# Differential attention with its scores as two 64-row tiles, query blocks that run on over the heads, a gathered rope, and the output gated from PSUM

## The reference, cut to what matters

```
aq, ak = rope_partial(a_q), rope_partial(a_k)      # 8 heads x 2 components x 64 dims, rope on the first 16 dims
s = einsum('bhcqd,bhckd->bhcqk', q, k) * 64 ** -0.5 # per head: two 1024 x 1024 score maps, contraction 64
p = softmax(s);  a = p[:, :, 0] - lam * p[:, :, 1]
o = a @ v                                           # v: 128 wide per head
o = rmsnorm(o, a_norm_g) * (1 - lam_init);  h_b = o * silu(a_z)
```

## Time and profile before

| | us |
|---|---|
| median of 3 runs | 1660.07 |
| the profiled execution, its own time | 1660.44 |
| its span on the core | 1658.4 |
| PE busy | 1600.7 (97%) |
| DVE, ACT, POOL busy | 985.6, 831.5, 542.7 |

### The profile page before, as it was taken

The page is one execution under the profiler, slowest core; times in us unless marked ns, Lnnn a source line. Parts: engine busy times, 40 slices in busy tenths (PEclk is TensorE's granted clock), DMA queues, the critical chain, the costliest instruction groups (busy, mean ns, idle before and its releaser), DMA issues.

```text
span 1658.4 us, 23808 instructions
## 1 busy us (share of the span) xinstructions
PE 1600.7 (97%) x8311; PEld 1338.9 (81%) x8311; DVE 985.6 (59%) x1607; ACT 831.5 (50%) x1474; POOL 542.7 (33%) x589
## 2 busy tenths in 40 slices
PE   6999999999999999999999999999999998999998
PEld 5788888888888878787777778787878887888898
DVE  6803774765665667777777777777776112334313
ACT  5314654654655654646464646555555234555312
POOL 4242152252161255151414233333310333333560
PEclk8999999999999999999999999999999999999999
DMA  5131021121121231212121212111211535432432
GB/s 164 34 121 39 26 88 39 55 72 38 51 74 29 66 87 29 58 32 58 32 57 32 57 32 57 32 44 32 53 60 32 181 114 165 152 92 86 127 102 102
DMA packets 130138, 116.08 MB, mean 70 GB/s; under 512 B 5210, under 2 KB 116379, under 8 KB 129060
## 3 DMA queue, kind: packets, MB, share of 16 engines
q1 hardware_dynamic: 125476, 102.78, 21.8%
q10 hardware_dynamic: 4608, 12.58, 2.0%
HBM read 85.96 MB, written 21.00 MB: 64 GB/s over the span
## 4 chain that ended last, share of the span: by engine, by line
PE 70%; DVE 10%; ACT 9%; issue 8%; DMA 2%; DVEq 0%; ACTq 0%; SPq 0%
PE ps L696 50%; PE ps L704 6%; PE ps L1002 6%; PE ps L908 2%; PE ps L900 2%; ACT aT_split L1903 2%; DVE aT_split L1437 2%; DMA k_stack<-k_stack 2%; DVE negmax L1432 2%; ACT probs L1898 1%; PE ps L785 1%; DVE state_f L1293 1%; ACT num L1801 1%; ACT w_split L1599 1%; PE ps L723 1%
## 5 line engine op out<-in xcount | busy, mean ns | idle before, releaser
L696 PE MATMUL ps<-xn_split,w_split 128*128 128x512 f32 x4224 | 1012.0, 396 | 0.4 <-DVE gate_cols L1198 0.4
L696 PEld LDWEIGHTS ps<-xn_split,w_split 128*128 128x128 f32 x4224 | 788.3, 189 | 166.6 <-DVE gate_cols L1198 0.6
L590 POOL TENSOR_TENSOR w_split<-w_raw,w_split 128x256 fp32r<-128x256 f32 x384 | 327.7, 884 | 956.9 <-ACT w_split L1599 956.3
L1898 ACT ACTIVATE probs<-ps,negmax 128x1024 f32<-128x1024 f32 x128 | 143.0, 1117 | 129.6 <-DVE negmax L1432 129.6
L1432 DVE TENSOR_REDUCE negmax<-ps 128x1 f32<-128x1024 f32 x128 | 150.0, 1212 | 2.4 <-PE ps L900 2.4
L1437 DVE TENSOR_TENSOR aT_split<-ps,aT_split 128x512 fp32r<-128x512 f32 x128 | 88.4, 691 | 100.8 <-ACT aT_split L1903 99.9
L900 PE MATMUL ps<-k_stack,q_stack 128*128 128x512 f32 x512 | 133.7, 403 | 2.8 <-DMA k_stack<-k_stack 2.7
L900 PEld LDWEIGHTS ps<-k_stack,q_stack 128*128 128x128 f32 x512 | 91.4, 188 | 20.9 <-issue 3.3
L704 PEld LDWEIGHTS ps<-aT_split,va_split 128*128 128x128 f32 x768 | 95.1, 190 | 10.6 <-issue 7.1
L704 PE MATMUL ps<-aT_split,va_split 128*128 128x256 f32 x768 | 98.8, 285 | 2.5 <-DVE aT_split L1437 1.9
L1599 ACT ACTIVATE w_split<-w_raw 128x1024 fp32r<-128x1024 f32 x94 | 98.9, 1052 | 0.2
(11 more groups left out here) (247 smaller groups left out, 1773.8 us busy)
## 6 DMA issues: line engine op xcount, KB each, us to landing
w_raw<-in_w_in SPq DMA_DIRECT2D x80, 512.0 KB, 3.9
k_stack<-k_stack SPq DMA_DIRECT2D x16, 512.0 KB, 4.2
qk_f<-spill_g SPq DMA_DIRECT2D x16, 512.0 KB, 3.6
spill_g<-qk_f ACTq DMA_DIRECT2D x12, 512.0 KB, 2.6
w_argument<-m_rows SPq DMA_DIRECT2D x8, 512.0 KB, 5.3
spill_m<-hT_f ACTq DMA_DIRECT2D x16, 256.0 KB, 2.2
spill_a<-o_out SPq DMA_DIRECT2D x32, 128.0 KB, 1.8
h_split<-spill_m SPq DMA_DIRECT2D x8, 512.0 KB, 5.0
```

What stands on the lines that cost most here:

```text
L590: lo = pool.tensor_tensor(wsp[b][:, 1, ks_], raw[b][:, ks_], wsp[b][:, 0, ks_].bitcast(F32), ALU.subtract)
L696: mm = pe.matmul(ps[:, half, :], wsp[b][:, wl, k, :], moving[:, xl, k, cols], start=(k == 0 and n == 0), stop=(k == KT - 1 and n == 2))
L1898: act.activation(pr[:, c], ps[:, 2 + 2 * c:4 + 2 * c, :].rearrange("p b k -> p (b k)"), ACT.Exp, bias=nmax[:, b, c:c + 1], accum_out=den[: ...
```

## The change

- Scores: `a_scores` (now also given which buffer) makes, per bank of 512 keys, three passes of high/low parts for each component, as matmuls over 64 rows: component 0 on partitions 0 to 63, component 1 on 64 to 127, one after the other into different banks. 12 matmuls per block, which wait for both exponentials of the block before.
- q and k are split whole (128 partitions at once) into two buffers each, one per parity of the head; the doubled copies and their DMA are gone. The loops over heads take two heads a turn.
- Order: the scores of the next head's block 0 stand in block 7 of this head. `fills` says how many steps of projection each block gets (10 and 6 in turn in a head that isn't the first), of which the first 3 stand between scores and the second round of transposes. Maxima and mixing of a head's block 0 go with its predecessor's block 7 on DVE and ACT.
- v's transposes go through banks 1 and 0 of the projections.
- Rope: four DMAs gather the 32 rows that turn from q (and from k) into a tile of 128 partitions x 2 x 128, POOL makes the rope on that, four DMAs give the rows back. cos and sin are loaded in that layout.
- Output: ACT squares it straight from PSUM, 1/rms is made in PSUM in place, DVE multiplies 1/rms, gain and gate, then the output from PSUM. The copy to `o_f32` is gone.
- Gate: its product is made by POOL in four pieces, the argument is clamped by DVE after block 0's work, and ACT's three steps stand at block 1. The mix's first half runs after the first exponential, its second half after the second.

```diff
+def fills(first):
+    return (0, 8) + tuple(8 + 14 * (q // 2) + 8 + 6 * (q % 2) for q in range(ST)) if first else \
+        (0, 0) + tuple(16 * (q // 2) + 10 + 6 * (q % 2) for q in range(ST))
+def halves(first, q):
+    at = fills(first)
+    return [n for n in range(8) if at[q + 1] < 8 * (n + 1) <= at[q + 2]]
...
-        qs = sb("q_stack", [P, 2, S], F32R, at=a_scope)
-        ks = sb("k_stack", [P, 2, 2, S], F32R, at=a_scope)
+        qs = [sb(f"aq_split{i}", [P, 2, S], F32R, at=a_scope) for i in range(2)]
+        ks = [sb(f"ak_split{i}", [P, 2, S], F32R, at=a_scope) for i in range(2)]
...
+            def turning(n, c, x):
+                rows = slice(c * AD + x * TURN, c * AD + (x + 1) * TURN)
+                return (qkf[rows, n].rearrange("i (b f) -> i b f", b=ST), turn_in[n][c * AD:(c + 1) * AD, x])
+            def gather(hh, n):
+                g, _ = tile_no(G_M, 8, MH - 1, 4 + n) if is_zero(hh) else tile_no(G_A, 4, hh - 1, n)
+                sp.wait_ge(proj_read, 2 * g + 2)
+                for c in range(2):
+                    for x in range(2):
+                        row, turn = turning(n, c, x)
+                        sp.dma_start(turn, row).then_inc(turn_gathered, 16)
+            def give_back(hh, n):
+                sp.wait_ge(turn_done, 4 * (2 * hh + n) + 4)
+                for c in range(2):
+                    for x in range(2):
+                        row, turn = turning(n, c, x)
+                        sp.dma_start(row, turn).then_inc(turn_returned[n], 16)
...
                 for j, c in enumerate((C_AQ, C_AK, C_AV, C_AZ)):
                     load_weights(G_A, 4, h, j, w_in_v, c + P + h * P)
-                    if j == (1 if first else 2):
-                        double_keys(h)
+                    if j < 2:
+                        gather(h, j)
+                        give_back(h, j)
                     if not first:
                         store_a(h - 1, j)
...
+                turn, own = 2 * hh + n, turn_in[n]
+                pool.wait_ge(turn_gathered, 64 * turn + 64)
+                pool.tensor_tensor(turn_cos, own, cos.unsqueeze(1).to_broadcast([P, 2, R_COLS]),
+                                   ALU.mult).then_inc(turn_done, 1)
+                for x in range(2):
+                    pool.tensor_tensor(turn_sin[:, x], own[:, 1 - x], sin[:, x], ALU.mult).then_inc(turn_done, 1)
+                pool.wait_ge(turn_done, 4 * turn + 3)
+                pool.tensor_tensor(own, turn_cos, turn_sin, ALU.add).then_inc(turn_done, 1)
+            def gate_product(h, first):
+                pool.wait_ge(a_gate_act.sem, a_gate_act.after(h, 2))
+                if not first:
+                    pool.wait_ge(a_ost.sem, a_ost.after(h, -1))
+                for n in range(QUARTERS):
+                    cols = slice(n * QUARTER, (n + 1) * QUARTER)
+                    g = pool.tensor_tensor(ga[:, cols], vz[:, 1, cols], aw[:, cols], ALU.mult)
+                g.then_inc(a_gate.sem, 1)
+            def a_tiles(h, first):
+                for j in range(3):
+                    split_weights(G_A, 4, h, j)
+                gate_product(h, first)
+                rope(h + 1, 0)
+                split_weights(G_A, 4, h, 3)
+                rope(h + 1, 1)
...
-            def a_scores(h, q):
+            def a_scores(h, par, q):
                 if q == 0:
-                    pe.wait_ge(k_doubled, 32 * h + 32)
-                    pe.wait_ge(a_qk_lo.sem, a_qk_lo.after(h, 3))
-                for c in range(2):
-                    if q > 0:
-                        pe.wait_ge(a_exp.sem, a_exp.after(h, 2 * (q - 1) + c))
-                    elif not is_zero(h):
-                        pe.wait_ge(a_exp.sem, a_exp.after(h, c) - 2)
-                    for i in range(2):
-                        for b in range(2):
-                            mm = pe.matmul(ps[:, 2 + 2 * c + i, :], qs[:, c, q * P:(q + 1) * P],
-                                           ks[:, c, b, i * HALF:(i + 1) * HALF], start=(b == 0), stop=(b == 1))
-                    mm.then_inc(a_score.sem, 1)
+                    pe.wait_ge(a_qk_lo.sem, a_qk_lo.after(h, 1))
+                if not (is_zero(h) and q == 0):
+                    pe.wait_ge(a_exp.sem, a_exp.after(h, 2 * q - 1))
+                for i in range(2):
+                    for n, (a, b) in enumerate(PASSES):
+                        for c in range(2):
+                            rows = slice(c * AD, (c + 1) * AD)
+                            mm = pe.matmul(ps[:, 2 + 2 * c + i, :], qs[par][rows, a, q * P:(q + 1) * P],
+                                           ks[par][rows, b, i * HALF:(i + 1) * HALF], start=(n == 0), stop=(n == 2))
+                            if i == 1 and n == 2:
+                                mm.then_inc(a_score.sem, 1)
...
+            def v_round(h, i, tile_half):
+                pe.wait_ge(proj_read, tile_half)
+                for n in range(4):
+                    c = 4 * i + n
+                    mm = pe.transpose(ps[:, 1 - i, n * P:(n + 1) * P], vz[:, 0, c * P:(c + 1) * P], ident[:])
+                mm.then_inc(a_vtr.sem, 1)
...
+            def a_head(h, par, first, last):
+                at = fills(first)
+                base, per_head, hh = (G_GL, 0, 0) if last else (G_A, 4, h)
+                def filler(begin, end):
+                    for n in range(8):
+                        lo, hi = max(begin, 8 * n), min(end, 8 * n + 8)
+                        if lo < hi:
+                            if lo == 8 * n and n in (1, 2):
+                                pe.wait_ge(a_vlo.sem, a_vlo.after(h, n - 1))
+                            proj_half(base, per_head, hh, n // 2, n % 2, begin=lo - 8 * n, end=hi - 8 * n)
+                read_by = 2 * (G_A + 4 * h)
                 if first:
+                    a_scores(h, par, 0)
+                    v_round(h, 0, read_by)
+                    filler(0, at[1])
                 for q in range(ST):
                     mix_round(h, q, 0)
                     if q + 1 < ST:
+                        a_scores(h, par, q + 1)
+                    elif not last:
+                        a_scores(h + 1, 1 - par, 0)
+                    if q == 0 and not first:
+                        v_round(h, 0, read_by)
+                    if q == (0 if first else 1):
+                        v_round(h, 1, read_by + 1)
+                    filler(at[q + 1], at[q + 1] + FIRST_PART)
                     mix_round(h, q, 1)
+                    if q == 0 and not first:
+                        squares(h - 1, 3)
                     if q % 2 == 0 and q > 0:
                         squares(h, q // 2 - 1)
+                    filler(at[q + 1] + FIRST_PART, at[q + 2])
                     if q % 2 == 1:
                         pv(h, q // 2)
+            a_head(0, 0, True, False)
+            with pe.Fori(0, AH // 2 - 1) as i:
+                a_head(2 * i + 1, 1, False, False)
+                a_head(2 * i + 2, 0, False, False)
+            a_head(AH - 1, 1, False, True)
...
+            def qk_low_a(hh, par, n):
+                dve.wait_ge(a_qk_hi.sem, a_qk_hi.after(hh, n))
+                dst = (qs, ks)[n][par]
+                dve.tensor_tensor(dst[:, 1], qkf[:, n], dst[:, 0].bitcast(F32), ALU.subtract).then_inc(a_qk_lo.sem, 1)
...
                 for q in range(ST):
+                    a_low_round(h, q, 0)
+                    nxt = (h, q + 1) if q + 1 < ST else None if last else (h + 1, 0)
+                    if nxt is not None:
+                        maxima(*nxt)
+                        mix_first(*nxt)
+                    a_low_round(h, q, 1)
+                    if q == 0 and not first:
+                        v_low_round(h, 0)
+                    if q == (0 if first else 1):
+                        v_low_round(h, 1)
+                    if nxt is not None:
+                        mix_second(*nxt)
                     if q == 0:
+                        dve.wait_ge(proj_read, 2 * (4 * h + G_A))
+                        if not first:
+                            dve.wait_ge(a_gate.sem, a_gate.after(h, -1))
+                        dve.tensor_scalar(aw, vz[:, 1], -1.0, LARGEST, ALU.mult, ALU.min).then_inc(a_clamped.sem, 1)
+                    if q == 1 and not first:
                         o_out_gate(h - 1, 3)
+                    if q in (3, 5, 7):
                         o_out_gate(h, q // 2 - 1)
+                    if q in (4, 6) and not last:
+                        qk_low_a(h + 1, 1 - par, q // 2 - 2)
...
                 for q in range(ST):
+                    nxt = (h, q + 1) if q + 1 < ST else None if last else (h + 1, 0)
+                    done = (h, q // 2 - 1) if q in (2, 4, 6) else (h - 1, 3) if q == 0 and not first else None
+                    high_round(h, q, 0)
+                    if done is not None:
+                        o_square(*done)
+                    if q == 0 and not first:
+                        v_high_round(h, 0)
```

(86 more changed lines are left out.)

364 lines of the change are left out of this document (119 added, 245 removed).

## The result

The changed kernel is slower: 1731.96 us, median of 4 runs (1729.56 to 1734.12), against 1658.62 us for the kernel before beside it; ratio 1.0443, 95% interval 1.0425 to 1.0461. Forecast were 1611 us and a range of 1589 to 1652.

What follows compares the result with a forecast made beforehand. TensorE's queue, busy 97% of the span, was taken to bound the kernel: 1660.4 - 29.6 (scores) - 35 (stops) + 17 (switches) - 1 (heads joined) = 1611.8, forecast 1611 us, range 1589 to 1652.

Steps and rivals of the forecast that it cites:

- (b): Stops within a head: filler between scores and second round of transposes leaves 1.0 of 5.4 us a head, -35 us.
- (e): Changed work of DVE, ACT, POOL and small DMAs, costed at nothing as lying beside TensorE's 78 us.
- (a): Scores: 512 matmuls of 128 rows become 384 pairs of 64 rows at 0.231 us a pair, -29.6 us.
- rival of serial pairs: Scores: the two 64-row matmuls run one after the other, 88.7 us over the forecast, 1700 us; chance 0.14.
- the one of loads that hold up the pairs: Scores: second tile's load not done beside the first's stream, +43 us, 1655 us; chance 0.06.
- (c): 128 switches between 128-row and 64-row work at 0.13 us each, +17 us.
- (d): Heads joined: next head's scores no longer wait at its start; 0.5 us ahead of head 0; -1 us.

Runs made afterwards that it cites:

- The three re-orderings: Kernel with gating moved early, with filler between the rounds, mix in halves and fillers of 10 and 6 all undone: 1641.32 us, ratio 0.9886.

## Why the prediction was wrong, point by point

- *The failed step is in (b), at the products with v.* I counted `pv`'s 2.89 us as cover for the mix, and never asked what `pv` itself waits for. The change swaps its wait from ACT's read (`a_rs`) to DVE's gating (`a_ost`), and the gating stands at the end of the odd block, behind the mix. That is readable in the code: `pv` of block 2n+1 wants what DVE does at the end of block 2n+1, ahead of which stand maxima and mix of block 2n+2. By the terms of (b) the price was there too: the mix ends 6.4 us after the scores, gating 0.9 later, 7.3, and `pv` was due 2.07 + 0.44 + 2.07 = 4.6 after them: 2.7 us, measured 2.3. The edit that its own title names, "gated from PSUM", I had put under (e), at nothing. Nor did I price that the change also puts the gating a block later. Moving the gating alone turned 1732 into 1620 us.
- *The clock wasn't in the sum.* No row of before had a stop of over 1 us within a head. But the trace of before shows elsewhere what a long one can do: in the tail TensorE stops for 4.6 us, and the granted clock of the next 4.6 us is 0.54. Here the clock took about a third of the loss.

```profile
1380.90 11.37 PE L696 MATMUL ps<-h_split,w_split 128*128 128x512 f32 x40 [4.64 <-DVE h_split L1507]
```

```profile
1380.90:1385.50 4.60, 4.60 (x12) 3.65 (x13) 0.00 (x0) 0.85 (x1) 0.93 (x2) 0.54 0.96 353
```

- *(a) was right as a mechanism*: pairs at one stream each, 12 matmuls in 1.58 us and not 2.8. The rival of serial pairs, which alone stood for "slower", is refuted, and so is the one of loads that hold up the pairs; the kernel was slower by a mechanism that no rival named.
- *(c) was too small*: 0.20 us a switch and not 0.13, 26 us and not 17. It lies within the bounds of 0 and 0.27 and nearer to the upper one, and eats nearly all of (a)'s 29.6 us. The Trainium skill's "Changing tiling mode (not just tile) drains the TensorE" ("TensorEngine Tiling (Array Packing)", Key Properties) gives no figure; that each switch costs 0.20 us here agrees with it.
- *The stops of (b), once gating is early*: work by the rows of before is 80.1 - 3.7 = 76.4 us a head, with switches 79.6; heads take 79.9. So 0.3 us of stops are left, not 1.0. The size was nearly right, the cause wrong: I gave it to the filler between the rounds, which alone is worth 5 us and in the kernel before less than nothing. The three re-orderings together carry 21 us, the rest of the change 18.
- *(d)*: the stops at the joined heads went, but TensorE's loop over a body of two heads costs 1.8 us at each of 2 turns, which I hadn't priced. The half us ahead of head 0 was not won: the first scores start at 603.2 as before, since TensorE, there 1.2 us earlier, waits 1.75 us for k's low part (DVE L1394), which (d) had hidden under the projections.
- With early gating the span is 1618.8, where (a) to (e) give 1609.8: + 9 for switches, + 3.6 for turns, + 1 for (d), - 5.6 for stops make 8 of the 9.

## What to carry to other kernels

When an edit drops a copy out of PSUM, the bank's release moves to the next reader: write down who releases each bank, and what stands ahead of that instruction in its engine's queue. Price every wait of the bounding engine anew, above all ahead of the work that the sum uses as cover. An engine that gets lighter (DVE, 65.7 to 57.7 us a head) can still become what everyone waits for, by order alone.

## What the runs showed of the hardware that I had not expected

- After 25 of 30 stops of 2.3 to 2.5 us TensorE ran for a while at the lower clock (in the one shown, granted 0.63 over the next 4.6 us), and 24 matmuls of 256 columns took 4.63 us instead of 3.04 to 3.13; after five it didn't, and the two stops of 1.6 and 1.8 us at the turns of the loop have no fall either. Useless matmuls in the stops made the kernel 35 us faster.
- Two 64-row matmuls on different rows run as one: in the changed kernel the two of a pair start 3 ns apart in the median and 20 at most, and 12 matmuls last 1.58 us, six streams and a switch. That holds (10 ns, 30 at most, and 1.59 us) also where the code lists three on one half of the rows and then three on the other. Going from 128-row to 64-row work or back costs 0.20 us.
- A hardware loop of TensorE whose body is two heads showed a stop of 1.6 to 1.8 us at each turn once nothing else waited there (1.2 us for both turns in the changed kernel); written out, it had none.
